# A one-core encoder step: who issues the first loads, in which order two projections finish their token tiles, and how the last attention heads are threaded

## The reference, cut to what matters

```python
for l in (0, 1):
    mod = silu(c) @ ada_w[l] + ada_b[l]                # shifts, scales and gates, 6 x 1024
    xm = rms(x) * g * (1 + scale1) + shift1
    y = mixer(xm) if l == 0 else diff_attention(xm, k_all, v_all)
    x = x + gate1 * y
    xm = rms(x) * g * (1 + scale2) + shift2
    x = x + gate2 * ((silu(xm @ w_gate) * (xm @ w_up)) @ w_down)
    if l == 0:
        k, v = rms(rms(x) @ w_k), rms(x) @ w_v         # shared keys and values

def diff_attention(...):                               # per head, in blocks of queries
    s = q @ k + bias; p = softmax(s)                   # two branches
    o = (p[0] - lam * p[1]) @ v
    return (rms(o) * (1 - lam_init)) @ w_o
```

## Time and profile before

| | us |
|---|---|
| median of 3 runs | 1481.31 (1481.21 to 1481.54) |
| the profiled execution's own time | 1480.78 |
| its span, first to last instruction | 1479.0 |
| PE busy in it | 1449.1 |
| PEld / DVE / POOL / ACT busy | 1370.1 / 1043.1 / 759.9 / 420.9 |

### The profile page before, as it was taken

The page is one execution under the profiler, slowest core; times in us unless marked ns, Lnnn a source line. Parts: engine busy times, 40 slices in busy tenths (PEclk is TensorE's granted clock), DMA queues, the critical chain, the costliest instruction groups (busy, mean ns, idle before and its releaser), DMA issues.

```text
span 1479.0 us, 29237 instructions
## 1 busy us (share of the span) xinstructions
PE 1449.1 (98%) x11236; PEld 1370.1 (93%) x11236; DVE 1043.1 (71%) x1890; ACT 420.9 (28%) x896; POOL 759.9 (51%) x512
## 2 busy tenths in 40 slices
PE   5999999999999999999999999999999999999999
PEld 4997899999999999999999777778999999999999
DVE  4897665567776877776676248896975779466698
ACT  4403454211110011112211147775321233111132
POOL 2445332655554455555444444566565556555554
PEclk9999999999999999999999999999999999999999
DMA  9573222244456544353322252230222222222222
GB/s 367 173 262 122 97 79 80 86 150 153 168 200 213 190 144 173 141 183 121 94 79 71 77 195 88 88 103 30 86 72 85 85 92 79 86 85 85 81 94 104
DMA packets 57531, 183.50 MB, mean 124 GB/s; under 512 B 6440, under 2 KB 9904, under 8 KB 57440
## 3 DMA queue, kind: packets, MB, share of 16 engines
q1 hardware_dynamic: 54528, 179.34, 35.0%
q10 hardware_dynamic: 2912, 2.92, 0.6%
HBM read 171.69 MB, written 10.55 MB: 123 GB/s over the span
## 4 chain that ended last, share of the span: by engine, by line
PE 88%; DVE 5%; issue 2%; POOL 1%; DMA 1%; ACT 1%; SPq 1%; ACTq 0%; POOLq 0%; DVEq 0%
PE psum L763 61%; PE psum L1035 7%; PE psum L829 7%; PE psum L1232 2%; PE psum L1167 1%; DMA ada_first<-in_ada_w 1%; PE psum L1324 1%; PE psum L1287 1%; PE psum L1041 1%; PE psum L1146 1%; DVE act_lo L1974 1%; DVE sc L2360 1%; PE psum L1274 1%; PE psum L977 1%; PE psum L800 1%
## 5 line engine op out<-in xcount | busy, mean ns | idle before, releaser
L644 POOL TENSOR_SCALAR w_hi<-raw 128x1024 fp32r<-128x1024 f32 (+1 forms) x168 | 192.7, 1147 | 575.9 <-PE psum L763 481.2
L648 POOL TENSOR_TENSOR w_lo<-raw,w_hi 128x1024 fp32r<-128x1024 f32 (+2 forms) x195 | 439.4, 2259 | 14.0
L763 PE MATMUL psum<-act_hi,w_hi 128*128 128x288 f32 (+1 forms) x1952 | 425.9, 299 | 1.1 <-issue 0.6
L763 PE MATMUL psum<-act_hi,w_lo 128*128 128x288 f32 (+1 forms) x1952 | 420.4, 297 | 0.0
L763 PE MATMUL psum<-act_lo,w_hi 128*128 128x288 f32 (+1 forms) x1952 | 420.2, 296 | 0.0
L763 PEld LDWEIGHTS psum<-act_hi,w_hi 128*128 128x128 f32 x1952 | 315.9, 190 | 7.0 <-issue 3.9
L763 PEld LDWEIGHTS psum<-act_hi,w_lo 128*128 128x128 f32 x1952 | 316.0, 189 | 0.0
L763 PEld LDWEIGHTS psum<-act_lo,w_hi 128*128 128x128 f32 x1952 | 315.3, 189 | 0.0
L763 PE MATMUL psum<-hid_both,w_hi 128*128 128x288 f32 x704 | 122.8, 297 | 0.0
L1921 DVE SCALAR_TENSOR_TENSOR psum<-ada_quad,cst,psum 128x512 f32<-128x512 f32 x168 | 112.8, 751 | 0.0
L763 PEld LDWEIGHTS psum<-hid_both,w_hi 128*128 128x128 f32 x704 | 103.5, 189 | 1.2 <-issue 1.2
(11 more groups left out here) (377 smaller groups left out, 2448.6 us busy)
## 6 DMA issues: line engine op xcount, KB each, us to landing
raw<-in_w_stream SPq DMA_DIRECT2D x153, 512.0 KB, 3.5
ada_quad<-in_ada_w SPq DMA_DIRECT2D x56, 512.0 KB, 4.5
raw<-in_w_down SPq DMA_DIRECT2D x32, 704.0 KB, 4.3
ada_first<-in_ada_w SPq DMA_DIRECT2D x8, 1024.0 KB, 14.2
ada_ring<-in_ada_w SPq DMA_DIRECT2D x14, 512.0 KB, 4.8
ada_more<-in_ada_w SPq DMA_DIRECT2D x10, 512.0 KB, 5.3
line_rep<-line SPq DMA_DIRECT2D x8, 352.0 KB, 4.6
line<-line_rep SPq DMA_DIRECT2D x8, 352.0 KB, 5.3
```

Of the source, the lines that this page charges most:

```text
L644: pool.tensor_scalar(hi, src, 1.0, 0.0, ALU.mult, ALU.add).then_inc(hi_split, 1)
L648: last = pool.tensor_tensor(lo[:, c:c + w], src[:, c:c + w], hi[:, c:c + w].bitcast(F32), ALU.subtract)
L763: last = mm(psum[:, b + half, 0:n_cols], weights[wp][:, k, :], parts[ap][:, k, half * HT:half * HT + n_cols], start=(k == 0 and n == 0), s ...
```

## The change

1. ScalarE issues the condition vector and the two line loads, at its very start. SP begins with x.
2. The three pieces of constants go behind the eight pairs and unit 2, on SP. The 1/D column is set by a memset on POOL instead, and PE's wait for the parameters before the first sums becomes a wait for that memset. Readers of the other constants wait for them (`consts_in`).
3. In the last unit of each half of a value projection the tokens' tiles are finished one by one, in the order 4, 0, 2, 1, 3. A new count `tile_done` lets ACT and DVE empty each tile when it is finished; tile 4's halves are added first. In the attention's second half `kq_scale` moves behind the emptying of tile 2.
4. Head 7's query projection is split as 8 matmuls over each of steps 25 to 30, and its `query_second` moves from step 29 to 30.
5. `oz_ready` is counted by both reads of the mean square. The transposes at a head's third step wait for the sample's read alone.
6. POOL splits unit 120 ahead of the refinement of head 6.
7. Unit 121's last four pieces run as (2,0), (3,0), (2,1), (3,1).

```diff
+V_ORDER = (4, 0, 2, 1, 3)
+        consts_in = 16 * (2 + 3)
+        def value_tile(eng, stage, nh, tt):
+            if tt == V_ORDER[-1]:
+                eng.wait_ge(unit_done, (U_V, U_AV)[stage] + 4 * nh + 4)
+            else:
+                eng.wait_ge(tile_done, 8 * stage + 4 * nh + tile_at[tt])
...
 # SP
-            sp.dma_start(cs_in, cond).then_inc(cond_ready, 16)
-            sp.dma_start(oh_sb[:, :], oh_line).then_inc(line_in, 16)
-            sp.dma_start(tab_sb[:, :], table).then_inc(line_in, 16)
             for c in range(4):
                 sp.dma_start(x[:, 2 * c:2 * c + 2, :], x_in[:, 2 * c:2 * c + 2, :]).then_inc(x_in_sem[c], 16)
-            for c0, c1 in ((C_ID, C_MEAN + 1), (C_BLK, C_HEAD), (C_OHC, NCONST)):
-                sp.dma_start(cst[:, c0:c1], consts[:, c0:c1]).then_inc(params_ready, 16)
             sp.dma_start(sml[:, :], small).then_inc(params_ready, 16)
...
             load_unit(2)
+            for c0, c1 in ((C_ID, C_MEAN), (C_BLK, C_HEAD), (C_OHC, NCONST)):
+                sp.dma_start(cst[:, c0:c1], consts[:, c0:c1]).then_inc(line_in, 16)
             load_pair(0)
...
 # POOL
+            pool.memset(cst[:, C_MEAN:C_MEAN + 1], 1.0 / D).then_inc(cs_zero, 1)
...
+                if h == H - 1:
+                    split_unit(U_AO + 3)
                 if h >= 1:
                     z, y, t, o = (tmp[:, n, :] for n in (1, 2, 3, 5))
...
-            split_unit(120)
             split_pairs(121, 2)
...
 # PE, project_values
-                        for kk in range(2):
-                            k = 2 * kp + kk
-                            for tt in range(TT):
+                        by_tile = kp == 3
+                        for kk, tt in [(kk, tt) for tt in V_ORDER for kk in range(2)] if by_tile else [(kk, tt) for kk in range(2) for tt in range(TT)]:
...
+                                if k == KT - 1 and tt != V_ORDER[-1]:
+                                    last.then_inc(tile_done, 1)
...
-            pe.wait_ge(params_ready, 64)
+            pe.wait_ge(cs_zero, 2)
...
 # PE, att_turn and the loop over g
                 elif qt == 2 and h >= 1:
-                    pe.wait_ge(oz_ready, h)
+                    pe.wait_ge(oz_ready, 2 * h - 1)
...
-                elif p + 2 < H and p >= 1:
+                elif p + 3 < H and p >= 1:
                     query_part(p + 2, *((0, 8), (8, 16), (16, 24), (24, 36), (36, 48))[s])
+                elif p == H - 3 or g == 5 * (H - 2):
+                    query_part(H - 1, 8 * (g - 5 * (H - 3)), 8 * (g - 5 * (H - 3)) + 8)
...
-            for k in range(4):
-                pe.wait_ge(lo_ready[A_O], 5 + k)
-                out_tile(4, 0, k, 4, k == 0, k == 3).then_inc(o_done, 1) if k == 3 else out_tile(4, 0, k, 4, k == 0)
-                last = out_tile(4, 1, k, 6, k == 0, k == 3)
+            for k, j in ((0, 0), (0, 1), (1, 0), (1, 1), (2, 0), (3, 0), (2, 1), (3, 1)):
+                if j == 0:
+                    pe.wait_ge(lo_ready[A_O], 5 + k)
+                last = out_tile(4, j, k, 4 + 2 * j, k == 0, k == 3)
+                if (k, j) == (3, 0):
+                    last.then_inc(o_done, 1)
...
 # ACT
+            sa.dma_start(cs_in, cond).then_inc(cond_ready, 16)
+            sa.dma_start(oh_sb[:, :], oh_line).then_inc(line_in, 16)
+            sa.dma_start(tab_sb[:, :], table).then_inc(line_in, 16)
...
             def mixer_values(nh):
-                sa.wait_ge(unit_done, U_V + 4 * nh + 4)
...
-                for tt in (0, 1, 4) if nh == 0 else (4, 0, 1):
+                for tt in (4, 0, 1):
+                    value_tile(sa, 0, nh, tt)
...
-                af(tmp[:, 1, TP:T], psum[:, 4, 448:512], ACT.Identity, bias=EPSC, scale=D / P)
+                af(tmp[:, 1, TP:T], psum[:, 4, 448:512], ACT.Identity, bias=EPSC, scale=D / P).then_inc(oz_ready, 1)
...
 # DVE
             def mixer_values(nh):
-                ve.wait_ge(unit_done, U_V + 4 * nh + 4)
-                for tt in (2, 3) if nh == 0 else (3, 2):
-                    last = ve.tensor_copy(vm[:, tt, 4 * nh:4 * nh + 4, 0:P], psum[:, tt, :].rearrange("p (h e) -> p h e", h=4))
-                last.then_inc(evac[1], 2)
                 ve.wait_ge(v_tail_lo, nh + 1)
                 own = vm[0:TS, 4, 4 * nh:4 * nh + 4, 0:P]
                 tt_(own, psum[0:TS, 4, :].rearrange("p (h e) -> p h e", h=4), own, ALU.add).then_inc(v_tail, 1)
+                for tt in (2, 3):
+                    value_tile(ve, 0, nh, tt)
+                    last = ve.tensor_copy(vm[:, tt, 4 * nh:4 * nh + 4, 0:P], psum[:, tt, :].rearrange("p (h e) -> p h e", h=4))
+                last.then_inc(evac[1], 2)
...
-                elif s == 4 and p + 2 < H:
+                elif s == 4 and p + 3 < H:
                     query_second(p + 2)
+                elif g == 5 * (H - 2):
+                    query_second(H - 1)
```

More of the change, by code:

```diff
@@ L318, in build @@
         v_tail, v_tail_lo, samples_ready = sem("v_tail"), sem("v_tail_lo"), sem("samples_ready")
+        tile_done = sem("tile_done")
+        tile_at = {tt: n + 1 for n, tt in enumerate(V_ORDER)}
         sq_ready, acc_done, ms_ready, ms_read, y0_ready, rstd_ready = (
@@ L609, in _ @@
                     sp.wait_ge(v_tail, 4)
+                    sp.wait_ge(evac[0], (U_AQ + 3) // 2)
                     for nh in range(2):
@@ L684, in _ @@
                     pool.wait_ge(oy_ready, h)
-                    pool.wait_ge(oz_ready, h)
+                    pool.wait_ge(oz_ready, 2 * h)
                     if 2 <= h <= 3:
@@ L893, in columns @@
                 pe.wait_ge(floor_ready, 1)
+                pe.wait_ge(line_in, consts_in)
                 for r, c in ((R_A, 0), (R_FLOOR, 40)):
@@ L1084, in ffn_last @@
                         project(f, 0, feed, shift=1, ready=ready, bank=4, k0=KT - 2)
-                        pe.wait_ge(oz_ready, H)
+                        pe.wait_ge(oz_ready, 2 * H)
                         pe.wait_ge(oy_ready, H)
@@ L1161, in att_scores @@
                     pe.wait_ge(v_tail, 4)
+                    wait_evac(pe, U_AQ + 3)
                 b = 2 * ((g + 1) % 2)
@@ L1243, in query_sums @@
                 if n >= 3:
-                    pe.wait_ge(oz_ready, n - 2)
+                    pe.wait_ge(oz_ready, 2 * n - 4)
                 mm(psum[:, 6, :], cst[:, C_BLK:C_BLK + P], ksq[:, 0:TP], start=True, stop=True)
@@ L1300, in att_sums @@
                 if h >= 1:
-                    pe.wait_ge(oz_ready, h)
+                    pe.wait_ge(oz_ready, 2 * h)
                 mm(psum[:, 6, :], mean_sq, tmp[:, 0, 0:TP], start=True, stop=True)
@@ L1473, in _ @@
             steps.wait()
+            sa.wait_ge(line_in, consts_in)
             af(row(R_T), row(R_T), ACT.Ln, bias=one_col[0:H]).then_inc(log_ready, 1)
@@ L1699, in att_values_out @@
             def att_values_out(nh):
-                sa.wait_ge(unit_done, U_AV + 4 * nh + 4)
-                for tt in (0, 1, 4) if nh == 0 else (0, 1, 4, 3):
+                for tt in (4, 0, 1) if nh == 0 else (4, 0, 1, 3):
+                    value_tile(sa, 1, nh, tt)
                     r = slice(0, P) if tt < 4 else slice(TS, P)
@@ L1773, in head_guess @@
             def head_guess(h):
-                sa.wait_ge(oz_ready, h + 1)
+                sa.wait_ge(oz_ready, 2 * h + 2)
                 steps(af(tmp[:, 2, :], tmp[:, 1, :], ACT.Ln))
@@ L2064, in _ @@
             ve.wait_ge(rstd_ready, 1)
-            ve.wait_ge(params_ready, 64)
+            ve.wait_ge(params_ready, 16)
             def first_modulation(m):
@@ L2102, in _ @@
             steps.wait()
+            ve.wait_ge(line_in, consts_in)
             for c0, c1 in ((0, TP), (TP, T)):
@@ L2390, in _ @@
             for nh in range(2):
-                ve.wait_ge(unit_done, U_AV + 4 * nh + 4)
-                if nh == 1:
-                    kq_scale(H, tmp[:, 0, :])
-                for tt in (2, 3) if nh == 0 else (2,):
-                    last = ts_(v_sb[nh][:, tt, :], psum[:, V_BANKS[nh][tt], :], rcol[:, tt:tt + 1], None, ALU.mult)
-                last.then_inc(evac[1], 2 - nh)
                 ve.wait_ge(v_tail_lo, nh + 3)
@@ L2399, in _ @@
                 stt(out=own, in0=psum[0:TS, V_BANKS[nh][4], :], scalar=rcol[0:TS, 4:5], in1=own, op0=ALU.mult, op1=ALU.add).then_inc(v_tail, 1)
+                for tt in (2, 3) if nh == 0 else (2,):
+                    value_tile(ve, 1, nh, tt)
+                    last = ts_(v_sb[nh][:, tt, :], psum[:, V_BANKS[nh][tt], :], rcol[:, tt:tt + 1], None, ALU.mult)
+                last.then_inc(evac[1], 2 - nh)
+                if nh == 1:
+                    ve.wait_ge(unit_done, U_AV + 8)
+                    kq_scale(H, tmp[:, 0, :])
             def query_first(n):
@@ L2514, in _ @@
             ve.wait_ge(oy_ready, H)
-            ve.wait_ge(oz_ready, H)
+            ve.wait_ge(oz_ready, 2 * H)
             ve.wait_ge(ov_ready, H - 1)
```

1 line of the change is left out of this document (added).

## The result

The changed kernel takes **1486.34 us** (median of 7 runs, 1485.07 to 1487.92) where the kernel before takes 1481.54 (7 runs, 1481.21 to 1481.95): a ratio of 1.0031, with a 95% interval of 1.0022 to 1.0041. It is slower by 4.8 us. The forecast was 1476.6 with a range from 1473.8 to 1479.1, so it was wrong, and in sign too. The profiled execution of the changed kernel took 1485.07 with a span of 1483.3; it stands 4.3 above the profiled execution before, whose span was 1479.0.

What follows compares the result with a forecast made beforehand. PE's matmuls were taken to bound the kernel, leaving about 30 us of stops to win. The seven parts summed to 4.65, say 4.7 us, off the 1481.31 median: 1476.6 us, range 1473.8 to 1479.1.

Steps and rivals of the forecast that it cites:

- Part 1's sum: Opening: x's loads start 1.38 us earlier and moving the constants saves 0.65; together 2.0 us gained, bounds 0 and 2.9.
- pair 3's landing still ends last: Opening: first pair's matmuls move from 18.35 to 16.7, 9.3 us before pair 3 was used, so its landing decides.
- Rival (c): Opening: the condition's loads race x and starve, first pair 5 us later; 1483.7 to 1485.3; chance 0.05.
- Part 2: Mixer's values, emptied by tile: 0.47 gained after the first half, 1.2 after the second; 1.65 taken, bounds 0.8 and 2.08.
- Part 3: Attention's values, emptied by tile: PE does query work while banks are emptied; 0 gained, range 0 to 0.5.
- Parts 4 and 5: Attention steps 30 and 34: PE arrives earlier, then waits for DVE; 0.2 (0 to 0.6) and 0.1 (0 to 0.6) gained.
- Part 6: Unit 120's split: a 0.64 us stop goes, slower DVE operations give back 0.45; 0.2 gained, bounds -0.3 and 0.64.
- The split fits there: Before head 6's refinement: unit 120's 3.6 us split fits POOL's 7.71 us idle time, so PE's 0.64 stop goes.
- Part 7: Unit 121: tile 0 released 1.6 us before the unit's end; PE's 0.53 us stop gained, bounds 0 and 0.6.
- (a): Opening: PE's own stop keeps its time, waiting 3.9 us instead of 1.85; gain 2.7, 1478.6; chance 0.2.
- (b): Opening: PE's 1.85 us stop and the half clock after it go; gain about 7.8, 1473.5; chance 0.12.
- The signs that were named: Wrong if first pair runs after 18.35, PE's "issue" stops pass 2 us, or last heads' weightings stretch over half a microsecond.

Runs made afterwards that it cites:

- line first: The changed kernel with only the line's two loads back on SP ahead of x, the condition staying on ScalarE: 1478.62 us.
- all small loads first: The changed kernel with the condition and the two line loads back on SP ahead of x: 1479.16 us.
- POOL waits: The changed kernel with POOL's first weight split waiting until DVE's additions of squares are done: 1482.29 us.
- pieces: The changed kernel with POOL making the low part of units 0 and 1 in four operations of 256 columns, not one of 1024: 1483.13 us.

## Why the prediction was wrong

**Part 1's sum (2.0 gained; 6.39 lost).** The step that failed is the sentence on the line: "the bias line must leave PSUM before DVE adds squares, and nothing of that is due for 10 us". The first half names the right dependence. The second is false by the trace of before: DVE's additions began at 7.61 there, 1.0 us behind the line's last copy (6.11+0.51=6.62). The line had 1.0 us of slack, and landed 4.1 later. The end of the squares (11.88) was read and taken for their beginning. With it fell the path on which the sum was built, "pair 3's landing still ends last": in the changed kernel the first pair itself runs at 25.62, 1.6 us after the time forecast for pair 3 (24.0). PE's own chain through the additions ended last, and no landing of a pair is in it. POOL's splits beside the additions, the second half of the loss, had no term in the sum.

**x and the constants.** The terms themselves were nearly right, as far as they can be read. Unit 0 was split from 11.83 on instead of 13.67, 1.84 earlier, where 2.0 was forecast. But that made the damage larger: the splits came forward to where the additions were going back. The gain of a transfer was counted, and not what its landing sets off on an engine that shares something with the late one. Even with the line first the two only just miss each other: the additions end at 7.01+5.11=12.12, and unit 0's split starts at 12.25. With all small loads first, where only the constants' bytes are left as a gain (0.65 forecast), the split starts at 12.96, 0.71 earlier than before. That the opening also ends 0.66 earlier there is partly luck, since its first pair runs 0.35 later than before, and the five executions with the line first end the opening anywhere from 44.38 to 45.50. Pair 3's landing can be read in the three of them whose weight loads waited for it: at 24.58 to 24.64 instead of 26.08, where x's 0.45 and the constants' 0.65 would make 24.98. (The upper bound of 2.9 for part 1 was mis-added: 1.38 and twice 0.65 are 2.7.)

**Rival (c), slower.** It gave the right sign and nearly the right size (1483.7 to 1485.3) at a chance of 0.05, with the wrong load, so the size is luck. The condition landed at 5.0, short of its point of 5.5. It cost about 0.9 us where nothing else held up DVE, and stood hidden behind the line in the changed kernel; the argument against it, that an 8 KB load among 16 engines gets its turn, is refuted by the rows: 4.2 us instead of 1.8, and 5.9 instead of 1.9 for 1 KB. The Trainium skill's rule that was cited (DMA: Bandwidth & Descriptors, Issuing engines are not separate DMA queues) says that such loads interleave on the same engines. That was read as "worth its issue time and no byte"; its other side, as these rows show it, is that a load issued beside a large one no longer goes ahead of it.

**Part 2 (1.65; 1.39).** Right in mechanism. The stop between the halves is gone (0.45 of 0.47); of the second, 0.94 of 1.2. PE still waited 0.7 us for DVE's last copy, not 0.4.

**Part 3 (0; 0.39).** PE had two short stops for the emptying of the attention's banks, 0.5 and 0.3 in the list of waits, and I had not looked for them:

```profile
PEld psum L829 <- ACT v_sb L1704: 0.5, 1, 0.5
...
PEld psum L829 <- DVE v_sb L2399: 0.3, 1, 0.3
```

They are gone in the changed kernel. In the bound of 0 to 0.5, but not the value taken.

**Parts 4 and 5 (0.2 and 0.1; 0.25 together by the offsets, about 0 each when undone).** The mechanism forecast, that PE arrives sooner and DVE makes it wait later, is what the runs show. The stop at step 30 fell further than the 1.3 forecast, to 0.37, and what it gave was gone by unit 120.

**Part 6 (0.2 gained; 0.80 lost).** Two steps failed. "The split fits there": of POOL's 7.71 us of idle time the first half could not be used, since unit 120's split waits until PE has finished unit 118 (`unit_done`), at 1020.9. It began at 1021.09, right ahead of the weighting. And the 0.36 per DVE operation came from the earlier trace rows, where POOL works in pieces of 256 columns, while unit 120 is split in one operation of 1024, 2.40 us long. A DVE operation waits for the end of the POOL operation that it meets, so the price goes by the length of that one: 1.21 for one weighting, not 0.36. That rule of the Trainium skill, cited in the prediction, gives this; the rows that I set against it were of short operations. And the 0.45 taken for the price was the low end of the 0.4 to 0.9 that was written down; its middle would have left no gain.

**Part 7 (0.53; 0.75).** Right: no wait for x at unit 121, and the last SwiGLU comes somewhat more than the stop sooner.

**Rivals (a) and (b), PE's own stop.** It neither stayed at its time nor went. It comes at the same matmul in every kernel and does not get shorter in step with a later arrival: 2.27 us from 29.46 (line first), 2.28 from 32.27 (POOL waits), 2.27 from 33.07 (pieces), 1.49 from 36.73 in the changed kernel; over all executions 0.76 to 2.56. So it moves with PE, on the whole, as the sum had it. Behind it there is a second stop of 0.9 to 1.8 us, some 7 us later, in the eight executions at full clock; in the four that ran at half clock behind the first, the kernel before among them, there is none (the one with the pieces had half the clock and a second stop of 0.62). With the line first, the two at full clock end the opening at 45.50 and 45.21, the three at half clock at 44.90, 44.38 and 44.99. So in these executions the half clock is not the loss that rival (b) made of it: where it was absent, the second stop mostly stood in its place. That is read from one execution of each kernel, and no run shows which of the two brings the other.

**The signs that were named.** Two of the three for being wrong came: the first pair ran later than 18.35 (25.62), and a weighting in the last heads stretched by over half a microsecond (1.21). The third, PE's own stops past 2 us, did not come in the changed kernel (1.49), but did in kernels that were faster than the one before (2.27 with the line first).

## What to carry to other kernels

Moving a small load to another engine's queue saves its issue time and gives up its place ahead of the large loads: ask what is the first use of each, and what is queued behind that use on its engine. Before a transfer is made to land earlier, look at what its landing sets off, and whether that engine shares something with one that is late. Where VectorE and GpSimd meet on the critical path, the price is the length of GpSimd's one operation; cutting it into pieces got back 3.2 us in the opening where holding it back got 4.1 (1483.13 and 1482.29 against 1486.34), and for unit 120 the pieces and the late split have the same median, 1477.16.

The version with the condition on ScalarE, the line's two loads on SP ahead of x, and unit 120 split late takes 1477.16 us, 0.9972 of the kernel before (0.9963 to 0.9982): the change with the two pieces taken out that the runs showed to cost time. That is 0.6 above the time forecast for the change whole.

## What the runs showed of the hardware that was not expected

- A 1 KB load took 5.9 us from issue to landing beside x's 2.3 MB on the other queue, and 1.9 us ahead of it; the 8 KB condition 4.2 instead of 1.8.
- A DVE addition of 0.77 us took 2.72 beside a POOL operation of 2.72, and a weighting of 0.55 took 1.76 beside one of 2.40. In pieces of 256 columns the same POOL work cost DVE's six additions 3.5 us less, and POOL itself 2.0 more.
- The clock at the same matmuls differed from execution to execution. Behind PE's first stop it was 1.00 in the execution with the line first and 0.50 (1.2 GHz) in the one that also splits unit 120 late, an edit that touches nothing in the opening; PE had stood still for 2.27 us before it in the one and 2.16 in the other. The two had parted before: from 18 to 20 us, at the first pairs, the clock was 1.00 in the one and 0.50 in the other. The windows from 32 to 34 us of the two (busy PE, PEld, DVE, ACT, POOL, clock, DMA share, GB/s):

```profile
32.00:34.00 2.00, 2.00 (x32) 1.84 (x32) 1.81 (x5) 1.15 (x2) 0.00 (x0) 1.00 1.02 410
```

```profile
32.00:34.00 2.00, 2.00 (x29) 1.72 (x31) 0.91 (x2) 1.51 (x3) 0.00 (x0) 0.50 1.02 408
```

What sets it, and what the stops wait for, stays open.
